# Operands in four transfers, the output weight in four steps and the zero rows in seven pieces, on the load queue of a hybrid decoder layer

## The chip, the core and the metric

The kernel runs on one core of a Trainium2 chip. It is one program in one launch, written in Bass: every engine has its own instruction stream, and semaphores order them. The metric is the device time of one execution in microseconds (us); lower is better.

## The reference, cut to what matters

One decoder layer over 1024 positions of width 1024, all in float32. An input projection feeds three groups of attention heads; their outputs go through one output projection, and a mixture of 32 experts follows.

```python
h = _rmsnorm(x, norm_attn[l])
proj = h @ w_in[l]
...
o_a = _nsa_mixer(nsa_q, kc, vc, ks_, vs_, kw, vw, nsa_g + b_gate[l], ...)
o_b = _fox_mixer(fq, fk, fv, ff + b_fgt[l])
o_c = _diff_mixer(dq, dk, dv, diff_lambda[l], diff_subln[l], _lambda_init(l))
x = x + jnp.concatenate([o_a, o_b, o_c], axis=-1) @ w_out[l]
x = x + _hier_moe(_rmsnorm(x, norm_ffn[l]), ...)
return _rmsnorm(x, norm_final)
```

`_nsa_mixer` has 8 heads with three branches each (compressed, selected, window), `_fox_mixer` 4 heads, `_diff_mixer` 4 heads with two maps each. In every branch a logit is `q . k` over 64 channels (32 in the last group), and a softmax over the allowed keys follows.

## The kernel before, in words

**Stages.** The input projection runs from 0 to about 305 us of the profile, attention from 305 to 733, the output projection with the router to 868, the experts to 1220, and the final gather and norm to the end. The projection is computed in 16 groups of 128 channels. Each group is written transposed to a scratch tensor `T_d` in DRAM, of shape 2 x 16 x 128 x 1024: index 0 holds the high part of each value and index 1 the low part. `T_r` is the same tensor seen as 2 x 2048 x 1024, so that a channel is a row of 4 KB.

**Units.** Attention is cut into 36 units of work in a fixed order: for each of eight heads X (selected), C (compressed) and Y (window), then four F, then eight D (two for each differential head). `PLAN.full` lists the 28 that are not C. The letter f counts them: X and Y alternate in f = 0 to 15, F is f = 16 to 19 and D is f = 20 to 27. Time is cut into slots: a unit X, Y, F or D holds six slots, a unit C one, so a head with X, C and Y takes 13. In a slot TensorE computes scores of the current unit (L1867, L1873, L1874), maxima of a later unit's scores (`max_pass`, L1834), values of an earlier slot (L1893) and at times transposes a row of shifts (`shift_T`, L1845). The maxima of a unit start nine slots before its own scores (`LEAD = 9`): four slots into the unit two before it in `PLAN.full`, and three slots where no C stands between. They need the unit's operands. Its scores need its row of shifts besides.

**Operands.** A unit X, Y or F has four tiles: `Q1`, 128 partitions, with the high part of q on partitions 0 to 63 and the low part on 64 to 127; `K1`, 128 partitions, with the high part of k twice; `Q2` and `K2`, with the high part of q and the low part of k on partitions 0 to 63. They exist three times (`x.set`) and once more for the first unit. `load_unit` fills them from `T_r` by six transfers of 64 rows, 256 KB each. A unit D has two tiles, filled by six transfers of 32 rows. The semaphore `ld_in` of a set counts 16 for each finished transfer, and `loaded(x)` is the count that `max_pass` waits for.

**The load queue.** SyncE (SP) issues all these transfers from one instruction stream, and they stand in one queue. Its loop over `PLAN.full` does, for each f: `shift_row(x)`, which waits for the maxima and then copies the 4 KB row of shifts into `Q2`, and for an X the same for its C; a wait until the unit before x has all its scores, then `load_unit(PLAN.full[f + 2])`; in the second unit of each D head one store of zero rows; and the store `O_d` of a finished head. At f = 4 it issues the output weight `wo` (tile `wraw`), 4 MB, as four transfers in a row. At f = 20 it issues two loads `ot` from `O_d`. `Y_d`, where the experts write, has 19 tiles of 96 rows that may stay unused and must be zero. Each of the four zero stores writes a quarter of the columns of all 19. `wo` is first read in the D units, the zero rows after the experts.

Before attention, one load of operands (the first unit's) and `K1y`, two transfers of 64 rows, stand in the same queue between the projection's stores to `T_d` and a load of projection weight, `wst`. ACT (`wth`, L872) and DVE (`wtl`, L1187) split `wst` before TensorE multiplies it (L1727).

Of the kernel before, what the change touches and what calls it, by code (L numbers as in the profile page):

```python
# [23 lines left out]
SEQ, D = 1024, 1024  # L24
# [3 lines left out]
HD = 64  # L28
# [7 lines left out]
CAP = 96  # L36
MAX_OVF = 2 * SEQ // (CAP + 1)
SURE = 2
NB = NE + SURE
# [141 lines left out]
def program(nc, a, out):  # L181
    f32, f32r = mybir.dt.float32, mybir.dt.float32r
# [4 lines left out]
    with ctx:  # L187
# [18 lines left out]
        def C(n, lo=0, hi=None):  # L206
# [67 lines left out]
        Q1, Q2, K1, K2 = ([at(f"{n}{u}", [P, SEQ], f32r, o + 4 * KB * k) for u, o in enumerate(SETS)]  # L274
                          for k, n in enumerate(("q1_", "q2_", "k1_", "k2_")))
# [11 lines left out]
        zrow = at("zrow", [P, D // 4], f32, ZE + 32 * KB)  # L287
# [3 lines left out]
        wraw = at("wraw", [P, KC, D], f32, ZD + 32 * KB)  # L291
# [60 lines left out]
        T_r = T_d.rearrange("a g p t -> a (g p) t")  # L352
# [3 lines left out]
        Y_d = nc.dram_tensor("Y_d", [NROWS, D], f32).ap()  # L356
# [40 lines left out]
        blk_zero = sem("blk_zero")  # L397
# [22 lines left out]
        yz_st = sem("yz_st")  # L420
# [54 lines left out]
        M_BANK, O_BANK = (4, 6), (5, 7)  # L475

        RS_D, RS_H, RS_K = 4, 5, 13
        ROUTES = ((0, 4, "0"), (4, 6, "1"), (6, 8, "2"))
        A_BATCH = ((0, 1), (1, 1), (2, 2), (4, 4))
        K_BATCH = ((0, 4), (4, 3), (7, 1))  # L480
# [47 lines left out]
        def _(sp_):  # L528
# [54 lines left out]
            def load_unit(x):  # L583

                if x.kind == "D":
                    q0, k0 = (HD * x.head + g * P + 32 * x.u for g in (G_QD, G_KD))
                    for b, (qp, kp_) in enumerate(((0, 0), (1, 0), (0, 1))):
                        for dst, part, r0 in ((Q2, qp, q0), (K2, kp_, k0)):
                            sp_.dma_start(dst[x.set][32 * b:32 * b + 32, :].bitcast(f32), T_r[part, r0:r0 + 32, :])\
                               .then_inc(ld_in[x.set], 16)  # L590
                    return
                if x.kind == "F":
                    q0, k0 = G_QF * P + HD * x.head, G_KF * P + HD * x.head
                else:
                    q0, k0 = G_QN * P + HD * x.head, (G_KS, G_KW)["XY".index(x.kind)] * P + HD * x.g
                for dst, half, part, r0 in ((Q1, 0, 0, q0), (Q1, 1, 1, q0), (K1, 0, 0, k0), (K1, 1, 0, k0),
                                            (Q2, 0, 0, q0), (K2, 0, 1, k0))[4 * (x.n == 2):]:
                    sp_.dma_start(dst[x.set][HD * half:HD * half + HD, :].bitcast(f32), T_r[part, r0:r0 + HD, :])\
                       .then_inc(ld_in[x.set], 16)

            def shift_row(x):
                row = 96 if x.kind in "CD" else HD
# [24 lines left out]
            for p in range(2):  # L627
                sp_.wait_ge(t_st[p], 32 * 8 + 1)

            stored = 0  # L630
            for f, x in enumerate(PLAN.full):
                if f:
                    shift_row(x)
                if f and x.kind == "X":
                    shift_row(PLAN.units[x.n + 1])
                if f >= 2 and f + 2 < len(PLAN.full):
                    sp_.wait_ge(s_ready, PLAN.units[x.n - 1].s_no[-1] + 1)
                    load_unit(PLAN.full[f + 2])
                if x.kind == "D" and x.u == 1:
                    sp_.wait_ge(blk_zero, 3)  # L640
                    c = slice(x.head * (D // 4), (x.head + 1) * (D // 4))
                    sp_.dma_start(Y_d[NB * CAP:, c].rearrange("(n p) d -> p n d", p=CAP),
                                  zrow[0:CAP].unsqueeze(1).broadcast_to([CAP, MAX_OVF - SURE, D // 4]))\
                       .then_inc(yz_st, 16)
                if f and PLAN.full[f - 1].kind in "YF":
                    sp_.wait_ge(oh_ready, stored + 1)
                    sp_.dma_start(O_v[:, :, HD * stored:HD * stored + HD], oh[:, stored % 2])\
                       .then_inc(oh_st[stored % 2], 16)
                    stored += 1
                    if stored == NSA_H + FOX_H:  # L650
                        for p in range(2):
                            sp_.wait_ge(oh_st[p], 16 * stored // 2)
                        for p in range(2):
                            sp_.dma_start(ot[:, p, :], O_d[p * P:(p + 1) * P, :]).then_inc(o_in[p], 16)
                if f == 4:
                    for c in range(4):
                        sp_.dma_start(wraw[:, 2 * c:2 * c + 2, :],
                                      a["wo"][c].rearrange("p (k n) -> p k n", k=2)).then_inc(wo_in, 16)

            def load_expert(e, q):  # L660
                sp_.dma_start(wgu[q][:], a["wgu"][e].rearrange("p (k n) -> p k n", k=KC)).then_inc(we_in[q], 16)
# [61 lines left out]
        def _(pool):  # L723
# [128 lines left out]

            for p in range(2):
                pool.wait_ge(y_st[p], 16 * NB // 2 + 1)
            pool.wait_ge(yz_st, 16 * 4)
            pool.wait_ge(ovf_y, 16 * n_ovf + 1)
            apart(pool)
            for t in range(NT):
# [11 lines left out]
        def _(act):  # L870
# [241 lines left out]
                if n:  # L1112
                    m_out(n - 1)
            m_out(NB - 1)
            act.wait_ge(yz_st, 16 * 4)
            act.wait_ge(y_st[0], 16 * NB // 2 + 1)
            n_ovf = act.value_load(info[0:1, 0:1], min_val=0, max_val=MAX_OVF - SURE)
            with act.Fori(0, MAX_OVF - SURE) as j:
# [573 lines left out]
        def _(pe_):  # L1692
# [112 lines left out]
            spread(5, 6)  # L1805
            def loaded(x):
                f = PLAN.full.index(x)
                return 96 * ((f - 1) // 3 + 1) - 64 * (x.set == 0) if f else 96

            def operands(x):  # L1810
                q1, k1 = (Q1[3], K1y) if x.n == 2 else (Q1[x.set], K1[x.set])
# [378 lines left out]
```

## Time and profile before

| | us |
|---|---|
| median of 3 runs | 1268.73 |
| lowest and highest of them | 1268.67, 1278.55 |
| the profiled execution, its own time | 1273.82 |
| span of its profile | 1271.9 |
| attention, 305 to 733, PE busy | 389.77 of 428.00 |
| experts, 868 to 1220, PE busy | 335.64 of 352.00 |

The span is what the profiler sees from the first to the last instruction; 1.9 us of the profiled execution lie around it. In the profile PE is TensorE's matmuls, PEld its weight loads, SPq the instructions by which SyncE issues transfers, q1 the hardware queue into which they go. PEclk is the granted clock of TensorE as a share of full speed. `q<-shr` is the copy of a row of shifts, `q<-T_d` and `k<-T_d` are loads of operands. The DMA view of a window gives the number of packets that started in it, how many of them are small, and for a queue its packets, MB and the share of 16 engines' time that they took.

### The profile page before, as it was taken

Reading aid. Unit: us, or ns where it says so; the run is one execution under the profiler, and the core shown is the slowest. Engines: PE = TensorE matmul, PEld = TensorE weight load, DVE = VectorE, ACT = ScalarE, POOL = GpSimd, SP = SyncE. Lnnn points to the kernel's source line nnn. Section 1 sums busy time; section 2 is a strip of 40 time slices with the busy share of each in tenths; the row PEclk is TensorE's granted clock in tenths of the full one; section 3 lists DMA queues with packets and bytes.
Section 4 is the critical chain, followed back from the end, with each engine's and each line's share of the span. In section 5 each row is a group of like instructions: output and inputs, shape, how many; then the busy total and the mean of one; then the engine's idle time right before and its main releaser. Section 6 shows DMA issues by size and latency. Waiting matters only on the chain.

```text
span 1271.9 us, 29600 instructions
## 1 busy us (share of the span) xinstructions
PE 1135.7 (89%) x12090; PEld 920.2 (72%) x12090; DVE 615.6 (48%) x1621; ACT 386.1 (30%) x691; POOL 188.0 (15%) x425
## 2 busy tenths in 40 slices
PE   6999899998998999999898889984999999999930
PEld 5989788786776778878676678874777777776710
DVE  4332345334665667665566443456343343344328
ACT  6411122222453555444565522220111111111103
POOL 1110000001211112111262200011110010011033
PEclk9999899999998999899988899996899999999975
DMA  8022654365455555444524343219899999999656
GB/s 338 17 83 97 209 182 149 117 182 146 97 139 185 120 118 118 109 110 95 159 76 141 100 164 103 91 52 358 301 393 377 389 391 378 373 390 386 232 188 258
DMA packets 69381, 251.58 MB, mean 198 GB/s; under 512 B 22176, under 2 KB 30272, under 8 KB 59392
## 3 DMA queue, kind: packets, MB, share of 16 engines
q1 hardware_dynamic: 59328, 219.53, 51.5%
q0 software_dynamic: 6112, 16.79, 3.9%
q10 hardware_dynamic: 3808, 13.37, 2.8%
q8 instruction: 98, 1.61, 0.5%
q14 instruction: 35, 0.29, 0.1%
HBM read 205.34 MB, written 49.15 MB: 200 GB/s over the span
## 4 chain that ended last, share of the span: by engine, by line
PE 75%; DMA 10%; DVE 8%; issue 3%; SPq 2%; ACT 1%; POOL 1%; POOLq 0%; DVEq 0%; ACTq 0%
PE PS L2036 14%; PE PS L1727 12%; PE PS L1893 10%; PE PS L2044 8%; PE PS L1973 7%; PE PS L1716 5%; PE PS L1834 4%; PE PS L1873 4%; PE PS L1874 3%; DMA wdn<-in_wdn 2%; DMA k<-T_d 2%; PE PS L2027 2%; PE PS L1867 2%; DMA q<-shr 2%; DMA wst<-in_wt 1%
## 5 line engine op out<-in xcount | busy, mean ns | idle before, releaser
L1032 ACT ACTIVATE pt<-PS,cst 128x512 f32<-128x512 f32 (+3 forms) x288 | 172.3, 649 | 167.2 <-PE PS L1874 122.2
L2036 PEld LDWEIGHTS PS<-XT,wgu 128*64 128x64 f32 x4352 | 184.5, 139 | 30.3 <-issue 29.3
L2036 PE MATMUL PS<-XT,wgu 128*64 128x96 f32 x4352 | 190.8, 249 | 4.7 <-issue 2.7
L1339 DVE CUSTOM_DVE_ANT_0 junkm<-PS,cst 128x512 f32<-128x512 f32 (+3 forms) x276 | 137.2, 532 | 94.0 <-PE PS L1834 90.9
L1893 PEld LDWEIGHTS PS<-V,pt 128*64 128x64 f32 x3840 | 137.2, 148 | 36.1 <-issue 22.5
L1893 PE MATMUL PS<-V,pt 128*64 128x65 f32 x3840 | 161.0, 237 | 0.0
L2044 PE MATMUL PS<-wdn,aT 128*96 128x512 f32 x272 | 122.5, 593 | 0.9 <-DVE YO L1638 0.9
L790 POOL TENSOR_SCALAR_AFFINE_SELECT pt<-pt 128x128 f32<-128x128 f32 x224 | 67.6, 304 | 269.9 <-ACT pt L1032 221.6
L1727 PE MATMUL PS<-hTh,wth 128*128 128x512 f32 x256 | 103.0, 402 | 4.6 <-DVE wtl L1187 4.6
L1834 PE MATMUL PS<-k,q 128*128 128x128 f32 (+3 forms) x324 | 92.4, 364 | 11.8 <-DMA k<-T_d 6.8
L1727 PE MATMUL PS<-hTh,wtl 128*128 128x512 f32 x256 | 100.7, 393 | 0.0
L1727 PE MATMUL PS<-hTl,wth 128*128 128x512 f32 x256 | 100.7, 393 | 0.0
L1873 PE MATMUL PS<-q,k 128*128 128x512 f32 (+1 forms) x228 | 88.8, 398 | 4.6 <-DMA q<-shr 4.6
L1624 DVE TENSOR_SCALAR ge<-PS 128x192 f32<-128x192 f32 x34 | 12.1, 357 | 160.8 <-PE PS L2036 160.7
L2044 PEld LDWEIGHTS PS<-wdn,aT 128*96 128x96 f32 x272 | 41.7, 163 | 56.1 <-issue 56.0
L1874 PE MATMUL PS<-q,k 65*128 65x512 f32 (+1 forms) x240 | 80.6, 353 | 0.0
L1834 PEld LDWEIGHTS PS<-k,q 128*128 128x128 f32 (+1 forms) x324 | 62.7, 204 | 21.3 <-DMA k<-T_d 7.8
L836 POOL DMA_INDIRECT XG<-h_d,ids x34 | 32.9, 968 | 296.2 <-PE PS L2027 273.6
L1096 ACT ACTIVATE ge<-ge 128x192 f32<-128x192 f32 x34 | 12.3, 363 | 188.6 <-DVE ge L1624 188.6
L1727 PEld LDWEIGHTS PS<-hTh,wth 128*128 128x128 f32 x256 | 48.7, 190 | 16.0 <-DVE wtl L1187 5.1
L1973 PE MATMUL PS<-woh,oth 128*128 128x512 f32 x128 | 51.9, 406 | 5.4 <-DVE otl L1440 4.8
L1727 PEld LDWEIGHTS PS<-hTl,wth 128*128 128x128 f32 x256 | 48.7, 190 | 10.8 <-issue 1.0
(262 smaller groups left out, 1618.2 us busy)
## 6 DMA issues: line engine op xcount, KB each, us to landing
wgu<-in_wgu SPq DMA_DIRECT2D x34, 2048.0 KB, 13.3
wdn<-in_wdn SPq DMA_DIRECT2D x34, 1024.0 KB, 19.6
q<-T_d SPq DMA_DIRECT2D x58, 256.0 KB, 4.7
k<-T_d SPq DMA_DIRECT2D x58, 256.0 KB, 5.6
Y_d<-YO ACTq DMA_DIRECT2D x34, 384.0 KB, 10.1
wst<-in_wt SPq DMA_DIRECT2D x16, 512.0 KB, 6.6
T_d<-thi SPq DMA_DIRECT2D x16, 512.0 KB, 2.6
T_d<-tlo SPq DMA_DIRECT2D x16, 512.0 KB, 3.9
```

The source lines that it names most:

```text
L790: ins = nc.gpsimd.affine_select(out=o, in_=o, compare_op=ALU.is_ge, fill=0.0, base=0, pattern=[[1, P]], channel_multiplier=-1)
L1032: ins = nc.scalar.activation(pt[:, (n + 2) % 6, 0:nt * P], PS[:, n % 4, 0:nt * P], ACT.Exp, scale=C("slopes", h, h + 1), bias=C("kb", w, w ...
L1339: V_.tensor_tensor_reduce(out=junk_[:, 0:L], in0=PS[:, bank, 0:L], in1=tab, scale=1.0, scalar=-3e38, op0=ALU.add, op1=ALU.max, accum_out=m ...
L1716: ins = mm(o, x[:, k, t * P:(t + 1) * P], wv[w][:, k, :], start=(k == 0 and x is hTh and w == 0), stop=(k == KC - 1 and w == 1))
L1727: ins = mm(PS[:, 2 * p + h, :], w[:, p, k * P:(k + 1) * P], x[:, k, h * 512:(h + 1) * 512], start=(k == 0 and w is wth and x is hTh), stop ...
L1834: ins = mm(PS[:, bank, 0:nk * P], q_[:, t * P:(t + 1) * P], k_[:, k0 * P:(k0 + nk) * P], start=True, stop=True)
L1873: mm(o, k1[:, j * P:(j + 1) * P], q1[:, q], start=True, stop=False)
L1874: ins = mm(o, k2[0:HD + 1, j * P:(j + 1) * P], q2[0:HD + 1, q], start=False, stop=True)
L1893: ins = mm(PS[h * HD:(h + 1) * HD, O_BANK[b % 2], (t % 4) * VW:(t % 4 + 1) * VW], pt[0:rows, (n + 2) % 6, q * P + h * HD:q * P + (h + 1) * ...
L1973: ins = mm(PS[:, 2 + h, :], x[:, t % 2, k, :], w[:, k, h * 512:(h + 1) * 512], start=(k == 0 and x is oth and w is woh), stop=(k == KC - 1 ...
L2036: ins = mm(PS[h * HD:(h + 1) * HD, 2 + p, f * CAP:(f + 1) * CAP], wgu[q][:, c, lo:lo + HD], XT[:, p, c, :], start=(c == 0 and f == 0), sto ...
L2044: ins = mm(PS[0:CAP, 5 + h, :], aT[:, p, c, :], wdn[q][:, c, h * 512:(h + 1) * 512], start=(c == 0), stop=(c == 1))
```

## The change

Three things change on SP's queue, and the counts that others wait for follow.

1. For X, Y and F, `Q1` is loaded by one transfer whose source is `T_r[:, q0:q0 + HD, :]`, 2 x 64 x 1024, and `K1` by one whose source is the 64 rows of k under a leading dimension of 2 with step 0. Both write 128 partitions. `Q2` and `K2` keep a transfer of 64 rows each. So 19 units take four transfers, not six. The first Y takes `Q2` and `K2` alone, as before; D units keep their six.
2. The output weight is issued in four steps of 1 MB, one in each of f = 4 to 7, after that unit's load.
3. The zero rows are stored in seven pieces of two or three tiles, one in each of f = 8 to 14, after that unit's load, and none in the D units.

```diff
                 else:
                     q0, k0 = G_QN * P + HD * x.head, (G_KS, G_KW)["XY".index(x.kind)] * P + HD * x.g
-                for dst, half, part, r0 in ((Q1, 0, 0, q0), (Q1, 1, 1, q0), (K1, 0, 0, k0), (K1, 1, 0, k0),
-                                            (Q2, 0, 0, q0), (K2, 0, 1, k0))[4 * (x.n == 2):]:
-                    sp_.dma_start(dst[x.set][HD * half:HD * half + HD, :].bitcast(f32), T_r[part, r0:r0 + HD, :])\
+                if x.n != 2:
+                    sp_.dma_start(Q1[x.set][:].bitcast(f32), T_r[:, q0:q0 + HD, :])\
                        .then_inc(ld_in[x.set], 16)
+                    sp_.dma_start(K1[x.set][:].bitcast(f32),
+                                  T_r[0:1, k0:k0 + HD, :].broadcast_to([2, HD, SEQ])).then_inc(ld_in[x.set], 16)
+                sp_.dma_start(Q2[x.set][0:HD, :].bitcast(f32), T_r[0, q0:q0 + HD, :]).then_inc(ld_in[x.set], 16)
+                sp_.dma_start(K2[x.set][0:HD, :].bitcast(f32), T_r[1, k0:k0 + HD, :]).then_inc(ld_in[x.set], 16)
...
+            def zero_rows(i):
+
+                n0, n1 = (NB + (MAX_OVF - SURE) * j // ZERO for j in (i, i + 1))
+                sp_.wait_ge(blk_zero, 3)
+                sp_.dma_start(Y_d[n0 * CAP:n1 * CAP, :].rearrange("(p r) (q d) -> p (r q) d", p=CAP, q=4),
+                              zrow[0:CAP].unsqueeze(1).broadcast_to([CAP, 4 * (n1 - n0), D // 4])).then_inc(yz_st, 16)
...
-                if x.kind == "D" and x.u == 1:
-                    sp_.wait_ge(blk_zero, 3)
-                    c = slice(x.head * (D // 4), (x.head + 1) * (D // 4))
-                    sp_.dma_start(Y_d[NB * CAP:, c].rearrange("(n p) d -> p n d", p=CAP),
-                                  zrow[0:CAP].unsqueeze(1).broadcast_to([CAP, MAX_OVF - SURE, D // 4]))\
-                       .then_inc(yz_st, 16)
+                if f in range(4, 8):
+                    sp_.dma_start(wraw[:, 2 * f - 8:2 * f - 6, :],
+                                  a["wo"][f - 4].rearrange("p (k n) -> p k n", k=2)).then_inc(wo_in, 16)
+                if f in range(8, 8 + ZERO):
+                    zero_rows(f - 8)
...
-                if f == 4:
-                    for c in range(4):
-                        sp_.dma_start(wraw[:, 2 * c:2 * c + 2, :],
-                                      a["wo"][c].rearrange("p (k n) -> p k n", k=2)).then_inc(wo_in, 16)
...
             def loaded(x):
                 f = PLAN.full.index(x)
-                return 96 * ((f - 1) // 3 + 1) - 64 * (x.set == 0) if f else 96
+                before = [y for y in PLAN.full[1:f + 1] if y.set == x.set]
+                return 16 * sum({"D": 6}.get(y.kind, 2 if y.n == 2 else 4) for y in before) if f else 64
```

The waits for the zero rows change from 16 x 4 to 16 x 7 in the same way.

The first place is SP's queue around the output weight, f = 4. `q_2_108` and `k_2_116` are `Q1` and `K1` of set 2, `q_2_112` and `k_2_120` its `Q2` and `K2`. Before:

```order
L605 DMA q_0_110<-shr 1x8x128 x2
L598 DMA q_2_108<-T_d 64x1024 x2
L598 DMA k_2_116<-T_d 64x1024 x2
L598 DMA q_2_112<-T_d 64x1024
L598 DMA k_2_120<-T_d 64x1024
L647 DMA O_d<-oh 128x8x64
L657 DMA wraw<-in_wo 128x2048 x4
L605 DMA q_1_111<-shr 1x8x128
```

After:

```order
L609 DMA q_0_110<-shr 1x8x128 x2
L598 DMA q_2_108<-T_d 128x1x1024
L600 DMA k_2_116<-T_d 128x1x1024
L602 DMA q_2_112<-T_d 64x1024
L603 DMA k_2_120<-T_d 64x1024
L651 DMA wraw<-in_wo 128x2048
L657 DMA O_d<-oh 128x8x64
L609 DMA q_1_111<-shr 1x8x128
```

The two pairs of 64-row transfers have become two transfers of 128 rows, and three quarters of the weight no longer stand ahead of the next row of shifts.

The second place is SP's queue around f = 8, the first with a piece of zero rows. Before:

```order
L605 DMA q_1_111<-shr 1x8x128 x2
L598 DMA q_0_106<-T_d 64x1024 x2
L598 DMA k_0_114<-T_d 64x1024 x2
L598 DMA q_0_110<-T_d 64x1024
L598 DMA k_0_118<-T_d 64x1024
L647 DMA O_d<-oh 128x8x64
L605 DMA q_2_112<-shr 1x8x128
```

After:

```order
L609 DMA q_1_111<-shr 1x8x128 x2
L598 DMA q_0_106<-T_d 128x1x1024
L600 DMA k_0_114<-T_d 128x1x1024
L602 DMA q_0_110<-T_d 64x1024
L603 DMA k_0_118<-T_d 64x1024
L638 DMA Y_d<-zrow 768x1x256
L657 DMA O_d<-oh 128x8x64
L609 DMA q_2_112<-shr 1x8x128
```

A store of 768 pieces of 1 KB now stands between the unit's load and the next row of shifts.

## Rows read from the trace of the kernel before

**Rows 1.** The page's chain that ended last, shares of the span.
```profile
PE 75%; DMA 10%; DVE 8%; issue 3%; SPq 2%; ACT 1%; POOL 1%; POOLq 0%; DVEq 0%; ACTq 0%
```

**Rows 2.** Two windows: busy time by engine, then PEclk, DMA share, GB/s.
```profile
305.00:733.00 428.00, 389.77 (x5163) 318.28 (x5162) 266.62 (x1010) 216.48 (x363) 103.64 (x281) 0.92 0.49 125
...
390.50:397.40 6.90, 6.50 (x57) 5.20 (x58) 3.21 (x13) 2.47 (x4) 1.17 (x4) 0.61 0.78 183
```

**Rows 3.** Waits of PE, 305 to 733: total, times, longest.
```profile
PE PS L1834 <- DMA k<-T_d: 6.8, 4, 3.9
...
PE PS L1867 <- DMA q<-shr: 6.4, 3, 4.0
...
PE PS L1873 <- DMA q<-shr: 4.6, 1, 4.6
```

**Rows 4.** PE's timeline, six places: start, duration, idle time before in brackets.
```profile
326.38 0.33 PE L1873 MATMUL PS<-q,K1y 128*128 128x128 f32 x1
...
390.90 0.48 PE L1873 MATMUL PS<-q,k 128*128 128x128 f32 x1 [4.61 <-DMA q<-shr]
...
554.55 0.33 PE L1834 MATMUL PS<-k,q 128*128 128x128 f32 x1 [1.43 <-DMA k<-T_d]
...
570.83 0.33 PE L1834 MATMUL PS<-k,q 128*128 128x128 f32 x1 [1.12 <-DMA k<-T_d]
...
584.89 0.33 PE L1834 MATMUL PS<-k,q 128*128 128x128 f32 x1 [0.33 <-DMA k<-T_d]
...
631.79 1.22 PE L1867 MATMUL PS<-q,k 97*128 97x512 f32 x2 [4.00 <-DMA q<-shr]
```

**Rows 5.** SP's timeline, the first issue of seven loads of operands.
```profile
253.17 1.98 SPq L598 DMA_DIRECT2D q<-T_d  x2
...
304.31 0.80 SPq L598 DMA_DIRECT2D q<-T_d  x1
...
438.43 1.14 SPq L598 DMA_DIRECT2D q<-T_d  x2
...
468.96 1.14 SPq L598 DMA_DIRECT2D q<-T_d  x2
...
544.99 1.24 SPq L598 DMA_DIRECT2D q<-T_d  x2
...
560.93 1.09 SPq L598 DMA_DIRECT2D q<-T_d  x2
...
575.78 1.10 SPq L598 DMA_DIRECT2D q<-T_d  x2
```

**Rows 6.** DMA in 480.7:483.4, 226:241, 590:595, 276:286 (q1), 452.8:464.
```profile
DMA packets 16, 0.00 MB, mean 2 GB/s; under 512 B 8, under 2 KB 16, under 8 KB 16
...
DMA packets 433, 1.58 MB, mean 105 GB/s; under 512 B 48, under 2 KB 48, under 8 KB 432
...
DMA packets 290, 0.81 MB, mean 162 GB/s; under 512 B 96, under 2 KB 96, under 8 KB 288
...
q1 hardware_dynamic: 288, 1.05, 26.2%
...
DMA packets 482, 1.60 MB, mean 143 GB/s; under 512 B 96, under 2 KB 96, under 8 KB 480
...
q1 hardware_dynamic: 480, 1.57, 61.7%
```

**Rows 7.** DMA in 743:756, and a small load's issue to landing.
```profile
q1 hardware_dynamic: 144, 0.52, 11.8%
...
pe<-in_pe SPq DMA_DIRECT2D x1, 16.0 KB, 1.9
```

**Rows 8.** ACT, DVE and PE around the next projection weight.
```profile
267.14 1.06 ACT L872 ACTIVATE wth<-wst 128x1024 fp32r<-128x1024 f32 x1 [2.25 <-DMA wst<-in_wt]
...
268.23 1.23 DVE L1187 TENSOR_TENSOR wtl<-wst,wth 128x1024 fp32r<-128x1024 f32 x1 [2.55 <-ACT wth L872]
...
276.10 0.79 PE L1727 MATMUL PS<-hTh,wth 128*128 128x512 f32 x1
```

More of the change, by code:

```diff
@@ L477, in program @@
         RS_D, RS_H, RS_K = 4, 5, 13
+        ZERO = 7
         ROUTES = ((0, 4, "0"), (4, 6, "1"), (6, 8, "2"))
@@ L854, in _ @@
                 pool.wait_ge(y_st[p], 16 * NB // 2 + 1)
-            pool.wait_ge(yz_st, 16 * 4)
+            pool.wait_ge(yz_st, 16 * ZERO)
             pool.wait_ge(ovf_y, 16 * n_ovf + 1)
@@ L1114, in _ @@
             m_out(NB - 1)
-            act.wait_ge(yz_st, 16 * 4)
+            act.wait_ge(yz_st, 16 * ZERO)
             act.wait_ge(y_st[0], 16 * NB // 2 + 1)
```

## The prediction

> **What bounds the kernel now.** I read the chain of waits first, then the windows by stage, then PE's waits in attention, then the timelines of PE and SP around them, and last the DMA counts of short windows. The chain says that matmuls set the end for 75% of the span and transfers for 10% [rows 1]. All three parts of the change act in attention, so only that stage counts. There PE is busy 389.77 of 428 us, at a mean granted clock of 0.92 [rows 2]. What the change can reach is the time in which PE waits for the load queue: 6.8 us in four waits for a unit's operands, 6.4 us in three waits for a row of shifts in the D units, and 4.6 us in one such wait behind the output weight [rows 3]. That is 17.8 us, plus what the clock loses after a long wait: in the 6.9 us behind the 4.61 us gap at 390.9 PEclk is 0.61 [rows 2, 4], so 0.39 x 6.9 = 2.7 us of work. I take 2.7 us for each wait of about 4 us or more.
>
> **How long a unit's load may take.** The load for f + 2 is issued when unit f starts, and PE wants it three slots later (four where a C lies between). For the last three X/Y/F loads the issues are at 544.99, 560.93 and 575.78 [rows 5], PE stood ready 1.43, 1.12 and 0.33 us before 554.55, 570.83 and 584.89 [rows 4], so it got there after 8.1, 8.8 and 8.8 us, and the loads took 9.6, 9.9 and 9.1 us. A head of 13 slots lasts 468.96 - 438.43 = 30.5 us [rows 5], 2.35 us a slot, so where a C lies between PE gets there after 8.6 + 2.35 = 10.9 us. This is the number to beat: a load slower than that is paid for in full, once for each unit, since the load behind it is not issued before the next unit starts.
>
> **Part 1, four transfers for six: how wide is a transfer?** The bytes are the same. What changes is the shape. Short windows of the DMA view tell how the queue cuts one. A row of shifts alone has 16 packets, 8 of them under 512 B; its 4 KB are described as 8 pieces, so 8 data packets and 8 small closing ones. Three transfers of 128 rows make 432 + 1 packets with 48 small ones, 16 each; six of 32 rows have 96 small ones, 16 each again [rows 6]. One closing packet for each DMA engine used fits all: 16 engines where the outermost count is 128 or 32, 8 where it is 8. The new sources have an outermost count of 2: two halves of `T_r` for `Q1`, a dimension of 2 with step 0 for `K1`. By this pattern each runs on 2 engines, though it writes 128 partitions. That is my choice for the sum, against a reading by the destination alone.
>
> The Trainium skill says the same as a rule, in "DMA: Bandwidth & Descriptors", section "Why a DMA increments its semaphore by 16 and not by 1": the number of engines is the largest up to 16 that divides the slowest non-1 dimension of both sides. The section "Rules for kernel authors" of that page names a leading zero-stride broadcast as the case that confines a transfer. By this rule the row of shifts has 8 and the new loads 2; the trace shows the 8, and nothing in it shows a 2.
>
> The pace of one engine: two stores of 128 rows keep 16 engines 26.2% of 10 us busy for 256 packets of 4 KB [rows 6], 0.164 us each. A load of 128 rows gives 11.8% of 13 us for 128 packets [rows 7], 0.192 us. The present loads of 64 rows give 61.7% of 11.2 us for 384 packets [rows 6], 0.288 us. Each of the two engines would move 64 packets for `Q1`, 64 for `K1` and 4 each for `Q2` and `K2`, 136 in all. I take 0.164 us, because only two engines run and nothing crowds them: 22.3 us, and 1.9 us from issue to landing of a load that is almost nothing [rows 7]. One unit's load: **24.2 us**.
>
> Now the sum. (a) Loads issued in f = 2 to 14: 24.2 - 10.9 + 2.7 = 16.0 us, 13 times, 208 us. (b) f = 15, 16, 17, which waited already: 24.2 less 9.6, 9.9 and 9.1, plus 2.7 each, 52 us. (c) The start: from 304.31 [rows 5] the two engines have the first Y's 8 packets and two loads of 136; the first Y's row of shifts stands behind them and lands at 304.3 + 1.9 + 280 x 0.164 = 352.1. PE began that unit at 326.38 [rows 4]: 25.7 us, and 2.7 for a second slow stretch. (d) The first unit's load at 253.17 [rows 5] stands ahead of `K1y` (8 packets) and `wst` (8) on those engines: 253.2 + 1.9 + 152 x 0.164 = 280.0, then 1.06 us for `wth` and 1.23 for `wtl`, 282.3 where PE went on at 276.10 [rows 8]: 6.2 us. SP saves some 1.2 us of issue in each unit, which nobody waits for: SP stands idle before each row of shifts. Part 1 costs 208 + 52 + 28.4 + 6.2 = **295 us**.
>
> The same skill, in "SBUF — State Buffer", section "Door 1: The DMA port swizzle", says that 64 partitions reach only half of the ports, and in "DMA: Bandwidth & Descriptors", section "Rules for kernel authors", that one transfer of 128 partitions beats two of half. The 0.288 against 0.164 us a packet agrees. Taken alone, this rule makes the change a gain; it is the first rival.
>
> **Part 2, the weight in four steps.** Three of its 4 MB no longer stand ahead of the row of shifts at f = 5. The wait of 4.6 us goes, and its slow stretch: -7.3 us. The pieces at f = 5, 6 and 7 cost nothing: 1 MB is 16 packets of 4 KB an engine, 2.6 us behind a load of 24.2, with the next load some 30 us later. Its reader comes in the D units, 200 us later. If the loads stayed short, 1 MB would land 2.6 us behind a load of 9 us, still inside the 15 us of a unit.
>
> **Part 3, the zero rows.** In the D units two waits go, 6.4 less the longest of 4.0 [rows 3], -2.4 us. The 4.0 us one ends at 631.79 [rows 4], in the first D units, where `ot` and `O_d` stand ahead of the row of shifts and no zero store has gone out; it stays. The seven pieces cost nothing for the reason given under part 2.
>
> Sum: 295 - 7.3 - 2.4 = 285 us. Against the profiled execution that is 1273.8 + 285 = 1559; that execution is 5.1 us over the median of the runs, so **1554 us**.
>
> **The rivals.** *Sixteen engines* (ends faster). If the destination's 128 partitions set the width, a unit has 16 packets an engine at 0.164 and 8 at 0.288, 4.9 us in place of 6.9. Then all four waits for operands go, 6.8 us with two slow stretches (5.4), though only the 3.9 us one is long; I count one stretch, 2.7. With parts 2 and 3: 6.8 + 2.7 + 7.3 + 2.4 = 19 us, 1250 us, between 1242 (more slow stretches go) and 1262 (VectorE is late next). The width decides: from 4 engines on a load (128 / 4 x 0.164 + 8 x 0.288 + 1.9 = 9.4 us) ends within 10.9 us. For it speaks that `wst` and all other loads of 128 partitions run on 16; against it, that none of them has a source cut differently from its destination. *Two engines at the crowded pace.* If reading `T_d` itself is what costs 0.288 us, a load takes 136 x 0.288 + 1.9 = 41.1 us: 16.9 us more in 16 units, 35 us more at the start, 19 in the projection, 1878 us. Against it: the packets differ between 64 and 128 partitions, not between tensors. *The change does less than it says*: the order of SP's instructions shows it done, so the only form of this is the first rival.
>
> **How the numbers follow.** Two engines near 0.164 us: 0.80, 1554 us. Crowded pace: 0.07. Sixteen engines: 0.13, of which 0.02 within 1%. About 1% is what a measurement of this kernel can tell from no change. The range: without any loss of clock, 18 x 2.7 = 49 us less, and a slot more of slack in some units, 1490; at 0.192 us a packet 61 us in the units, 8 at the start, 4 in the projection, and a full half clock for 6.9 us (0.75 us more each), 1640. The other cases lie far outside and hold 0.20.
>
> **What the profile of the changed kernel would show.** Right: `q<-T_d` and `k<-T_d` of 512 KB that land after 12 to 24 us; a window with one such load with 2 small packets for each of its two wide transfers; a DMA share near 0.15 through attention; PE waiting some 13 us in each of 16 units, for `k<-T_d` or `q<-T_d`; a head of about 62 us; no wait of PE for a row of shifts at f = 5; the stages from 733 on unchanged in length. Wrong: wide loads that land in 5 us, 16 small packets each, PE busy above 0.93 in attention. With 4 or 8 small packets a transfer the time would lie near the first rival's.

## The result and the profile after

The changed kernel takes 1593.65 us (median of 4 runs, 1590.67 to 1597.07) against 1269.30 (4 runs, 1268.67 to 1278.55): a ratio of 1.2535, 95% interval 1.2471 to 1.2599. It is a quarter slower. Its profiled execution took 1595.02 us, with a span of 1593.1.

The page first: PE's busy time, then the chain that ended last by engine and by line.

```profile
PE 1184.2 (74%) x12090; PEld 956.1 (60%) x12090; DVE 617.5 (39%) x1621; ACT 386.4 (24%) x691; POOL 187.8 (12%) x425
...
PE 54%; DMA 24%; SPq 13%; DVE 5%; issue 3%; ACT 1%; POOL 1%; POOLq 0%; DVEq 0%; ACTq 0%
DMA k<-T_d 18%; PE PS L2043 11%; SPq L602 10%; PE PS L1733 9%; PE PS L2051 7%; PE PS L1980 6%; PE PS L1900 5%; PE PS L1722 4%; PE PS L1841 3%; DMA wdn<-in_wdn 2%; PE PS L2034 2%; DMA q<-shr 1%; PE PS L1874 1%; DMA wst<-in_wt 1%; PE PS L1880 1%
```

The chain answers to [rows 1]: PE fell from 75% to 54%, transfers rose from 10% to 24%, and SPq from 2% to 13%. Two entries are new and large, the load `k<-T_d` and SP's own issue of a load in L602 (`Q2`). PE did the same 12090 matmuls in 1184.2 us, not in 1135.7; the lower granted clock behind the waits, shown below, accounts for the 48.5 us.

PE's waits from 300 to 1054 us, the attention stage of the changed kernel (L1841 is the old L1834, L1874 and L1880 are L1867 and L1873):

```profile
PE PS L1841 <- DMA k<-T_d: 260.8, 17, 18.4
```

These answer to [rows 3]. The wait for a unit's operands went from 6.8 us in 4 to 260.8 us in 17. That is one for each of the sixteen units loaded in f = 2 to 17, and one at the start.

PE's timeline at five places:

```profile
287.46 0.77 PE L1733 MATMUL PS<-hTh,wth 128*128 128x512 f32 x1 [11.95 <-issue]
...
369.89 0.47 PE L1880 MATMUL PS<-q,K1y 128*128 128x128 f32 x1 [14.83 <-DMA q<-shr]
...
415.72 0.80 PE L1841 MATMUL PS<-k,q 128*128 128x128 f32 x2 [16.28 <-DMA k<-T_d]
...
910.13 0.48 PE L1841 MATMUL PS<-k,q 128*128 128x128 f32 x1 [17.93 <-DMA k<-T_d]
...
956.93 0.73 PE L1874 MATMUL PS<-q,k 97*128 97x512 f32 x2 [1.37 <-DMA q<-shr]
```

They answer to [rows 4] and [rows 8]. The projection's matmul of 276.10 comes at 287.46, the first Y of 326.38 at 369.89, the last X/Y/F maxima of 584.89 at 910.13. The row of shifts behind the weight, a wait of 4.61 us before, is not waited for: the only wait of L1880 is the first Y's. The one at f = 21 went from 4.00 to 1.37.

SP's timeline of one load (f = 2), the DMA view inside it, 391.5 to 398.9 us, and the packets of the whole next load (f = 3), 422.6 to 449.6 us:

```profile
389.30 0.55 SPq L598 DMA_DIRECT2D q<-T_d  x1
389.90 0.53 SPq L600 DMA_DIRECT2D k<-T_d  x1
390.47 7.90 SPq L602 DMA_DIRECT2D q<-T_d  x1
398.41 0.60 SPq L603 DMA_DIRECT2D k<-T_d  x1
```

```profile
q1 hardware_dynamic: 94, 0.39, 12.9%
...
DMA packets 437, 1.59 MB, mean 59 GB/s; under 512 B 44, under 2 KB 52, under 8 KB 436
```

Ninety-four packets of 4 KB in 7.4 us, at 12.9% of 16 engines, are two engines (12.5%) that never pause, at 0.16 us a packet (two engines x 7.4 us / 94). The second row has 44 small packets: 16 each for `Q2` and `K2` and 8 for the row of shifts make 40, which leaves two for each wide transfer. The four issues should take 0.6 us each; the third takes 7.90. That is what put SPq into the chain. In f = 8 to 14, where a piece of zero rows follows the load, SP's next issue behind the piece (`O_d` or a row of shifts) is held as well, for 5.9 to 12.0 us in six of the seven. From the first issue at 389.30 to PE's start at 415.72 the load takes 26.4 us.

Windows: a busy stretch and a waiting one, then two stretches behind waits, then the stage behind attention. Columns as in [rows 2].

```profile
391.00:399.00 8.00, 8.00 (x127) 6.77 (x126) 5.43 (x23) 4.51 (x8) 1.17 (x4) 1.00 0.13 52
440.00:448.00 8.00, 0.00 (x0) 0.00 (x0) 0.00 (x0) 0.00 (x0) 0.00 (x0) 0.50 0.13 51
...
415.70:419.70 4.00, 3.98 (x37) 3.46 (x37) 1.01 (x5) 0.70 (x2) 0.07 (x1) 0.50 0.02 4
...
453.50:457.50 4.00, 4.00 (x24) 2.75 (x24) 2.47 (x9) 1.67 (x3) 0.56 (x2) 0.50 0.09 33
...
1054.00:1189.00 135.00, 121.98 (x663) 104.40 (x662) 61.74 (x143) 28.98 (x65) 10.61 (x43) 0.94 0.33 121
```

The transfer share is 0.13 in both of the first two stretches, whether PE works or waits: two engines of 16. In the waiting stretch no engine computes. The granted clock is 0.50, the lower of its two levels (1.2 GHz), in the last part of the wait and in the stretches behind it. Over the 12 us behind each of the sixteen waits it is 0.59 to 0.86, so the lower level lasts 3.4 to 9.8 us there. The stages after attention are 135 and 352 us long as before: all of the loss lies ahead of 1054.

### The profile page after: what moved, and what is told of

Read it like the earlier page. It is cut to its first block, busy times and chain, and to the rows that moved or that the text cites. A ratio compares the mean times of both kernels' runs of the same rounds, so it can differ in the third digit from the quotient of the medians.

```text
span 1593.1 us, 29565 instructions
## 1 busy us (share of the span) xinstructions
PE 1184.2 (74%) x12090; PEld 956.1 (60%) x12090; DVE 617.5 (39%) x1621; ACT 386.4 (24%) x691; POOL 187.8 (12%) x425
## 4 chain that ended last, share of the span: by engine, by line
PE 54%; DMA 24%; SPq 13%; DVE 5%; issue 3%; ACT 1%; POOL 1%; POOLq 0%; DVEq 0%; ACTq 0%
DMA k<-T_d 18%; PE PS L2043 11%; SPq L602 10%; PE PS L1733 9%; PE PS L2051 7%; PE PS L1980 6%; PE PS L1900 5%; PE PS L1722 4%; PE PS L1841 3%; DMA wdn<-in_wdn 2%; PE PS L2034 2%; DMA q<-shr 1%; PE PS L1874 1%; DMA wst<-in_wt 1%; PE PS L1880 1%
## 5 line engine op out<-in xcount | busy, mean ns | idle before, releaser
L1841 PE MATMUL PS<-k,q 128*128 128x128 f32 (+3 forms) x324 | 104.0, 402 | 266.0 <-DMA k<-T_d 260.8
L1841 PEld LDWEIGHTS PS<-k,q 128*128 128x128 f32 (+1 forms) x324 | 67.6, 226 | 280.1 <-DMA k<-T_d 266.2
L1900 PE MATMUL PS<-V,pt 128*64 128x65 f32 x3840 | 177.0, 252 | 0.0
L1900 PEld LDWEIGHTS PS<-V,pt 128*64 128x64 f32 x3840 | 151.8, 161 | 40.7 <-issue 23.6
L1733 PE MATMUL PS<-hTh,wth 128*128 128x512 f32 x256 | 103.1, 403 | 16.4 <-issue 11.9
L1880 PE MATMUL PS<-q,k 128*128 128x512 f32 (+1 forms) x228 | 95.0, 422 | 0.0
L1881 PE MATMUL PS<-q,k 65*128 65x512 f32 (+1 forms) x240 | 87.4, 381 | 0.0
L1630 DVE TENSOR_SCALAR ge<-PS 128x192 f32<-128x192 f32 x34 | 12.2, 358 | 162.2 <-PE PS L2043 162.2
L1345 DVE CUSTOM_DVE_ANT_0 junkm<-PS,FX 128x512 f32<-128x512 f32 (+3 forms) x48 | 25.5, 556 | 88.8 <-PE PS L1844 74.1
L1881 PEld LDWEIGHTS PS<-q,k 65*128 65x128 f32 x240 | 54.2, 226 | 3.7 <-issue 0.2
```

What stands on the lines that cost most here:

```text
L1345: V_.tensor_tensor_reduce(out=junk_[:, 0:L], in0=PS[:, bank, 0:L], in1=tab, scale=1.0, scalar=-3e38, op0=ALU.add, op1=ALU.max, accum_out=m ...
L1733: ins = mm(PS[:, 2 * p + h, :], w[:, p, k * P:(k + 1) * P], x[:, k, h * 512:(h + 1) * 512], start=(k == 0 and w is wth and x is hTh), stop ...
L1841: ins = mm(PS[:, bank, 0:nk * P], q_[:, t * P:(t + 1) * P], k_[:, k0 * P:(k0 + nk) * P], start=True, stop=True)
L1880: mm(o, k1[:, j * P:(j + 1) * P], q1[:, q], start=True, stop=False)
L1881: ins = mm(o, k2[0:HD + 1, j * P:(j + 1) * P], q2[0:HD + 1, q], start=False, stop=True)
L1900: ins = mm(PS[h * HD:(h + 1) * HD, O_BANK[b % 2], (t % 4) * VW:(t % 4 + 1) * VW], pt[0:rows, (n + 2) % 6, q * P + h * HD:q * P + (h + 1) * ...
```

## The experiments

All ratios are to the kernel before, run on the same chip: 1272.39 us (17 runs, 1268.86 to 1277.62) beside the first four kernels, 1272.43 (17 runs, 1266.25 to 1278.49) beside the others.

### widths: one transfer at a time, by the shape of its source

```python
one(T["whole"][:], wt[0])
one(T["sixteen"][:], wt[0:16, 0:P // 16, :])    # eight, four, two in the same way
one(T["twins"][:], wt[0:1, 0:HD, :].broadcast_to([2, HD, SEQ]))
one(T["pairs"][:], wt[0, 0:HD, :].unsqueeze(1).broadcast_to([HD, 2, SEQ]))
one(T["half"][0:HD, :], wt[1, 0:HD, :])
...
sp_.dma_start(T["fst"][:], wt[0:2, 0:HD, :]).then_inc(late, 16)
sp_.dma_start(T["snd"][:], wt[2:4, 0:HD, :]).then_inc(late, 16)
sp_.dma_start(T["trd"][0:HD, :], wt[5, 0:HD, :]).then_inc(late, 16)
```

> Leaves the whole layer out: SP alone loads 512 KB tiles one after another, each waited for, with sources whose outermost count is 128, 16, 8, 4 and 2, twice over, then the step-0 source of the change (2 x 64) and the same rows as 64 x 2, a load of 64 rows and one of 32. Width theory: at 0.16 us a 4 KB packet and some 2 us of fixed time, 16 and 128 land in about 3.3 us, 8 in 4.6, 4 in 7.1, 2 in 12.2; the step-0 source of 2 x 64 in 12.2, the 64 x 2 one in 3.3 to 4.5. Rival (the destination sets the width, and the time of the change comes from the size or from reading T_d): all of 512 KB land within 1 us of each other. Then a 4 KB row behind a wide load and behind a narrow one: by the width theory it lands about 3 us after its issue in the first case, 10 to 12 in the second. Last, two narrow loads and a third load in a row: if SP's long third issue is the queue being full, the third issue takes about 8 us here too, with nothing else going on.

SP's timeline, the second round and what follows it; each transfer of the round is waited for before the next is issued, so the distance to the next row is its time from issue to landing.

```profile
58.27 0.35 SPq L197 DMA_DIRECT2D whole<-in_wt  x1
61.64 0.58 SPq L197 DMA_DIRECT2D sixteen<-in_wt  x1
66.15 0.66 SPq L197 DMA_DIRECT2D eight<-in_wt  x1
72.57 0.56 SPq L197 DMA_DIRECT2D four<-in_wt  x1
81.06 0.52 SPq L197 DMA_DIRECT2D two<-in_wt  x1
93.75 0.51 SPq L197 DMA_DIRECT2D twins<-in_wt  x1
106.23 0.57 SPq L197 DMA_DIRECT2D pairs<-in_wt  x1
109.94 0.51 SPq L197 DMA_DIRECT2D half<-in_wt  x1
113.29 0.34 SPq L197 DMA_DIRECT2D quarter<-in_wt  x1
...
115.97 0.29 SPq L197 DMA_DIRECT2D brow<-in_wt  x1
118.94 0.56 SPq L213 DMA_DIRECT2D bnarrow<-in_wt  x1
119.55 0.48 SPq L197 DMA_DIRECT2D brow<-in_wt  x1
131.69 0.51 SPq L217 DMA_DIRECT2D fst<-in_wt  x1
...
132.80 8.39 SPq L219 DMA_DIRECT2D trd<-in_wt  x1
156.25 18.81 SPq L197 DMA_DIRECT2D out<-whole  x8
```

The packets of `two`, 81 to 93.7 us, and those from 131.0 to 131.3 us:

```profile
DMA packets 130, 0.52 MB, mean 41 GB/s; under 512 B 2, under 2 KB 2, under 8 KB 130
...
DMA packets 5, 0.01 MB, mean 27 GB/s; under 512 B 3, under 2 KB 3, under 8 KB 5
```

The same 512 KB into the same 128 partitions take 3.4 us from 128 source rows, 8.5 from a source whose outermost dimension is 4, and 12.7 and 12.5 where it is 2, as two halves of a tensor (`two`) or as a dimension with step 0 (`twins`). With 64 outermost and the step of 0 inside (`pairs`) they take 3.7. So it is the source's outermost dimension, not the destination's partitions, and the price is what two engines take: 64 x 0.164 + 1.9 = 12.4 us. Two of the 130 packets of `two` are small, one closing packet for each engine. The Trainium skill says of `two` and `twins` what the rows show ("DMA: Bandwidth & Descriptors", section "Why a DMA increments its semaphore by 16 and not by 1"): the number of engines must divide the slowest dimension of both sides.

Three things stand beside this. A 4 KB row behind a wide transfer lands within 3.0 us (115.97 to 118.94). Behind a narrow one it takes 11.5 to 12.1: SP waits for both transfers, until 131.69, and the only small packets of the two, two of the narrow transfer and one of the row, start between 131.0 and 131.3, against the row's issue at 119.55. A third transfer behind two narrow ones holds SP for 8.39 us in its issue, though nothing else runs: the same hold as in L602. With those 64 rows behind them the two narrow transfers have all landed 24.6 us after the first issue (131.69 to 156.25).

### interleaved: the same four transfers on 16 engines

```diff
-                    sp_.dma_start(Q1[x.set][:].bitcast(f32), T_r[:, q0:q0 + HD, :])\
+                    sp_.dma_start(Q1[x.set][:].bitcast(f32), T_r[:, q0:q0 + HD, :].rearrange("a c t -> c a t"))\
...
-                                  T_r[0:1, k0:k0 + HD, :].broadcast_to([2, HD, SEQ])).then_inc(ld_in[x.set], 16)
+                                  T_r[0, k0:k0 + HD, :].unsqueeze(1).broadcast_to([HD, 2, SEQ]))\
```

Channel c now lies on partitions 2c and 2c + 1 instead of c and c + 64; `K1y` (now one transfer, not two) and the compressed keys, which meet the same `Q1`, are laid out the same way, with four more small matmuls and two more small copies on ACT.

> The changed kernel with the same four transfers of the same bytes, but Q1, K1 and K1y hold their 128 partitions as 64 channels x 2 (high and low, or twice the same), so that the outermost count of each source is 64. The compressed keys follow the new order of channels. Width theory: 16 engines, a unit's load lands in some 5 us, no wait of PE for operands, 1250 us, between 1242 and 1262. Rival (a large transfer is slow by itself, or SP's long issue holds the rows back): near 1590 us, as the changed kernel.

1257.49 us (5 runs), ratio 0.9879, interval 0.9854 to 0.9903. The page's issues (KB each, median us to landing), then PE's waits from 305 to 760 us:

```profile
q<-T_d SPq DMA_DIRECT2D x19, 512.0 KB, 4.1
k<-T_d SPq DMA_DIRECT2D x19, 512.0 KB, 5.5
```

```profile
PE PS L1845 <- DMA k<-T_d: 3.0, 2, 2.9
```

For a unit these are the same bytes, the same number of transfers and the same partitions: 336 us faster than the changed kernel and 1.2% faster than the one before. The width is the whole loss. With it restored, the change is the gain that the prediction's first rival gave (1250, from 1242 to 1262).

### steps_only: parts 2 and 3 without part 1

Six transfers a unit as before; the weight in four steps and the zero rows in seven pieces, as in the diff of the change.

> The kernel before with the output weight in four steps and the zero rows in seven pieces, the loads still six transfers of 64 rows. My sum says -7.3 us for the weight and -2.4 for the zero rows: 1259 us, ratio 0.992. Rival (pieces between the units delay rows of shifts or loads): 1269 or above, with new waits of PE for q<-shr or k<-T_d in f = 8 to 14.

1266.01 us (12 runs, 1257.83 to 1269.86), ratio 0.9943, interval 0.9922 to 0.9964. No wait for a row of shifts is left behind the weight. There is now one wait of 0.9 us for POOL's `pt`, and waits for operands are 7.3 us in 5 (4.0 the longest), 6.8 before. At f = 21 PE waits 1.08 us where it waited 4.00, and one wait for a row of shifts, of 1.75 us at 707.14, is left in the D units.

### q1_narrow: only Q1 on two engines

```diff
-                    sp_.dma_start(K1[x.set][:].bitcast(f32),
-                                  T_r[0:1, k0:k0 + HD, :].broadcast_to([2, HD, SEQ])).then_inc(ld_in[x.set], 16)
+                    for half in range(2):
+                        sp_.dma_start(K1[x.set][HD * half:HD * half + HD, :].bitcast(f32), T_r[0, k0:k0 + HD, :])\
+                           .then_inc(ld_in[x.set], 16)
```

> The changed kernel with K1 loaded by two transfers of 64 rows again, so that only Q1 comes by a narrow one: 64 packets on two engines, not 128. Width theory: a load lands in 1.7 + 10.1 + 4.6 = 16.4 us, 5.5 over what PE allows, so with the clock 8 us more in each of 13 units, 10 in three, 12 at the start: about 1405 us, near the middle between 1259 and 1594. Rival (the step 0 of K1's source is what is slow): near 1260 us. Rival (any narrow transfer stops SP's queue): near 1590.

1451.74 us (2 runs), ratio 1.1406, interval 1.1366 to 1.1446: some 47 us over what I expected. The first issue of two loads on SP (f = 5, beside a piece of the weight, and f = 8, without one) and PE's start behind each:

```profile
444.64 0.55 SPq L598 DMA_DIRECT2D q<-T_d  x1
...
521.33 0.53 SPq L598 DMA_DIRECT2D q<-T_d  x1
```

```profile
465.61 0.80 PE L1842 MATMUL PS<-k,q 128*128 128x128 f32 x2 [8.86 <-DMA k<-T_d]
...
539.93 0.79 PE L1842 MATMUL PS<-k,q 128*128 128x128 f32 x2 [7.76 <-DMA k<-T_d]
```

They take 21.0 and 18.6 us. The four loads beside pieces of the weight take 20.3 to 21.0, the other twelve 18.4 to 19.2, not the 16.4 of my count of packets. Half the narrow bytes cost 57% of the loss (0.1527 of 0.2656 in ratio, counted from interleaved), where the expectation had 44% (1405 of 1259 to 1594). The likely reason is that transfers which run at the same time slow these packets, as the longer loads beside the weight show; for the other twelve it is not tested. In the units no issue of the load's own transfers is long. SP is held at the start, behind two narrow transfers (11.95 us at 317.08, a half of `K1`), and for 5.5 to 8.7 us at four stores `O_d` that stand behind a piece of zero rows with one narrow transfer ahead. In interleaved, with the same pieces, no issue of SP between 245 and 760 us takes over 2.5 us.

### part1_only: part 1 without parts 2 and 3

The loads of the changed kernel; the weight at once at f = 4 and the zero rows in the D units, as before.

> The kernel before with part 1 alone: the four narrow transfers of a unit; the output weight goes out at once at f = 4 and the zero rows in the D units, as before. Theory (parts 2 and 3 only pay where loads are short; under loads of 27 us their waits lie in PE's wait for operands, and the pieces of the weight at f = 4 to 7 even lengthen the loads beside them by 1 to 2 us): 1588 to 1596 us, the same as the change within its scatter; the load at f = 5 to 7 takes 26 to 27 us from its first issue to PE's start, not 28 to 29, with one longer one behind the 4 MB of the weight. Rival (the parts add up, as the prediction's sum had it): 1594 + 7.3 + 2.4 = 1603 us, with a wait of PE for a row of shifts of 4 us or more at f = 5.

1596.00 us (4 runs, 1588.57 to 1597.74), ratio 1.2531, interval 1.2492 to 1.2569: the changed kernel's time. SP's issue of the weight and of the next load (f = 5), and PE's start behind it:

```profile
464.79 13.02 SPq L660 DMA_DIRECT2D wraw<-in_wo  x4
...
488.88 0.54 SPq L597 DMA_DIRECT2D q<-T_d  x1
```

```profile
515.13 0.80 PE L1838 MATMUL PS<-k,q 128*128 128x128 f32 x2 [11.19 <-DMA k<-T_d]
```

The loads at f = 5, 6 and 7 take 26.3, 26.6 and 26.7 us, in the changed kernel 29.1, 28.1 and 28.2: the pieces of the weight lengthen the load beside them by 1.5 to 2.8 us. All sixteen loads have a mean of 26.7 us here, against 26.9 in the changed kernel. The wait for the row of shifts at f = 5 is 0.92 us, not 4 or more. The additive sum (1603) falls with it: under loads of 27 us parts 2 and 3 give nothing that can be measured, within the 0.3 to 0.6% of the two intervals.

### interleaved_only: the wide loads without parts 2 and 3

> The kernel before with Q1 and K1 loaded by one transfer each whose source has 64 rows outermost and the two parts inside them; the weight in one go and the zero rows in the D units, as before. Theory (the wide loads take 4 to 5 us instead of 9 and remove only the waits for operands; parts 2 and 3 take the 4.6 us wait behind the weight by themselves): ratio to before 0.992 to 0.996, about 1264 us; steps alone gave 0.994 and both together 0.988, so the two add up. PE still waits 4 us for the row of shifts at f = 5, and hardly for k<-T_d. Rival (the two gains are the same one, a queue less full): 0.988, 1257 us, as with both.

1267.64 us (12 runs, 1262.09 to 1272.07), ratio 0.9955, interval 0.9935 to 0.9976. PE's wait behind the weight, from 380 to 400 us, is as long as before:

```profile
PE PS L1881 <- DMA q<-shr: 4.3, 1, 4.3
```

A wait for operands of 2.95 us stands at 553.84, which I had not expected. 0.9955 x 0.9943 is 0.9898, against 0.9879 with both and an interval that holds it. On short loads the two gains add: some 6 us from the wide transfers, some 7 from parts 2 and 3.

### q2_first: the changed kernel with Q2 and K2 issued first

```diff
+                sp_.dma_start(Q2[x.set][0:HD, :].bitcast(f32), T_r[0, q0:q0 + HD, :]).then_inc(ld_in[x.set], 16)
+                sp_.dma_start(K2[x.set][0:HD, :].bitcast(f32), T_r[1, k0:k0 + HD, :]).then_inc(ld_in[x.set], 16)
                 if x.n != 2:
...
-                sp_.dma_start(Q2[x.set][0:HD, :].bitcast(f32), T_r[0, q0:q0 + HD, :]).then_inc(ld_in[x.set], 16)
-                sp_.dma_start(K2[x.set][0:HD, :].bitcast(f32), T_r[1, k0:k0 + HD, :]).then_inc(ld_in[x.set], 16)
```

> The changed kernel with Q2 and K2 issued ahead of the wide-destination loads Q1 and K1; nothing else moves. Theory (two 64-row transfers on 16 engines crowd the first narrow one or wait behind both of them on the two engines; with them first, the two engines have only Q1 and K1 left, which end together): a load takes 24.5 to 26 us from its first issue to PE's start instead of 26.9, so 1560 to 1585 us; SP's 8 us issue goes away, since no third transfer meets the two narrow ones before the row of shifts. Rival (the load is the two engines' 128 to 136 packets whatever the order): 1594 us within 0.5%. In both, if the long issue moves to the row of shifts behind the load, it is the third transfer after two narrow ones that holds SP, whatever it is.

1556.39 us (4 runs, 1551.88 to 1562.37), ratio 1.2254, interval 1.2217 to 1.2292. Nothing but the order differs, and 37 us are back. SP's timeline of the load at f = 4 with its piece of the weight, then PE's start behind it and behind the load at f = 8:

```profile
445.00 0.50 SPq L597 DMA_DIRECT2D q<-T_d  x1
...
446.79 0.53 SPq L602 DMA_DIRECT2D k<-T_d  x1
447.37 9.09 SPq L651 DMA_DIRECT2D wraw<-in_wo  x1
...
570.04 0.50 SPq L597 DMA_DIRECT2D q<-T_d  x1
```

```profile
471.41 0.80 PE L1841 MATMUL PS<-k,q 128*128 128x128 f32 x2 [15.36 <-DMA k<-T_d]
...
594.51 0.79 PE L1841 MATMUL PS<-k,q 128*128 128x128 f32 x2 [11.44 <-DMA k<-T_d]
```

The hold of 9.09 us moved to the piece of weight, the first transfer behind the two narrow ones. In nine of the eleven loads behind which a piece of the weight or of the zero rows follows at once, that piece is held for 8.1 to 9.3 us, in the other two (f = 12 and 13) for 2.1 and 2.2. A load takes 25.0 us in the mean of the sixteen (26.4 here, beside a piece of the weight; 24.5 at f = 8), against 26.9 in the changed kernel.

### interleaved_moved: two moves on SP's queue for what is left

The interleaved kernel, with the load for f = 2 (the second head's X) ahead of that for f = 1 (the first Y), and the two loads `ot` one unit later, behind that unit's load.

```diff
-            for x in PLAN.full[1:4]:
+            for x in (PLAN.full[2], PLAN.full[1], PLAN.full[3]):
...
+                if f == 21:
+                    for p in range(2):
+                        sp_.wait_ge(oh_st[p], 16 * stored // 2)
+                    for p in range(2):
+                        sp_.dma_start(ot[:, p, :], O_d[p * P:(p + 1) * P, :]).then_inc(o_in[p], 16)
...
```

> The interleaved kernel (16 engines for Q1 and K1, weight in four steps, zero rows in seven pieces), with two moves on SP's queue: at the start the load of the first X ahead of that for the Y before it, and the two loads ot from O_d moved one unit later, behind that unit's load. Theory (the two waits that are left in attention, 2.9 us for k<-T_d at 315 us and 1.1 us for the row of shifts at f = 21, come from what stands ahead in the queue): 1251 to 1254 us, 4 to 6 us below the interleaved kernel. Rival (another engine is late next there, or the wait for the first Y's operands takes the place): 1257 us, no difference.

1255.51 us (4 runs, 1253.45 to 1256.91), ratio 0.9872, interval 0.9845 to 0.9898. The intervals of the two interleaved kernels overlap nearly whole, so a gain is not shown. PE's starts on the maxima of f = 2, interleaved and then moved, each with a later wait for a row of shifts:

```profile
315.04 0.50 PE L1845 MATMUL PS<-k,q 128*128 128x128 f32 x2 [2.86 <-DMA k<-T_d]
...
695.88 0.73 PE L1878 MATMUL PS<-q,k 97*128 97x512 f32 x2 [1.74 <-DMA q<-shr]
```

```profile
315.25 0.49 PE L1845 MATMUL PS<-k,q 128*128 128x128 f32 x2 [2.44 <-DMA k<-T_d]
...
693.40 0.73 PE L1878 MATMUL PS<-q,k 97*128 97x512 f32 x2 [1.69 <-DMA q<-shr]
```

The load for f = 2 was issued 1.5 us earlier (303.16, not 304.64), and PE still starts at the same time. Ten transfers go out within 7 us there; why the place among them did not decide was not tested. The wait of 1.1 us at f = 21 is gone with `ot` moved. The one of 1.7 us for a later row of shifts was there before the move and stays.

## Why the prediction was right, and where it was off

The forecast was 1554 us in a range of 1490 to 1640; the kernel takes 1593.65. Its main mechanism held: the new sources run on two engines, and each unit pays for it in full. It was 40 us low, and by the profiles the sum was 285 where 321.2 was found (1593.1 - 1271.9). By its own steps:

| stretch | predicted | measured |
|---|---|---|
| up to the first Y's scores, (c) and (d) | +34.6 | 369.89 - 326.38 = +43.5 |
| from there to the last wait for operands, (a), (b), part 2 | 208 + 52 - 7.3 = +252.7 | 910.13 - 584.89 - 43.5 = +281.7 |
| the rest, part 3 | -2.4 | -4.0 |

**Width** (right). Two engines, from the count of closing packets: DMA share 0.13, and a transfer alone takes 12.5 us. The pace of 0.164 us a packet was right too, 0.16 here. Choosing it over the crowded 0.288 decided between 1554 and 1878. The new shape in a trace could be told from the closing packets of the old ones.

**The load, 24.2 us** (mis-sized). It measured 26.9, the mean of 16 from first issue to PE's start (25.6 to 29.1; 26.4 at f = 2). The term holds for the two engines alone: in widths two narrow transfers and 64 rows behind them, on a chip with nothing else to do, landed in 24.6 us. The prediction had nothing for what the transfers beside them cost. q2_first gives 1.8 of the 2.7 us back by order alone; where the rest goes is open. The pieces of the weight account for 1.5 to 2.8 us of three loads, but hardly for the mean, which is 26.7 without them (part1_only). The step that said that these pieces "cost nothing" under a load of 24.2 us was wrong all the same. In q1_narrow loads were 2.0 to 4.6 us over the count of packets.

**The clock, 2.7 us for each long wait** (mis-sized, and right in total by luck). PE's busy time rose by 48.5 us, 18 x 2.7 = 49 predicted. But the mean clock in the 12 us behind the sixteen waits is 0.715, which is 3.4 us of work lost at each, and the 48.5 us are a net: the slow stretches behind the waits of the kernel before (0.61 behind 390.9) are in its busy time.

The longer loads did not come through in full either: 16 x 2.7 us make 43, but PE's waits in the sixteen units are 242 us where the sum had 217 (13 x 13.3 and, for the last three, 44). The difference lies in what PE does between a load's first issue and its wait. The sum had 10.9 us for f = 2 to 14; it measures 12.4 in the mean. Two rows of the kernel before (448.32, behind the issue of 438.43) and of the changed one (481.08 less the wait, behind the issue of 453.45):

```profile
448.32 0.40 PE L1834 MATMUL PS<-k,q 128*128 128x128 f32 x2
```

```profile
481.08 0.80 PE L1841 MATMUL PS<-k,q 128*128 128x128 f32 x2 [14.82 <-DMA k<-T_d]
```

That is 9.9 us before and 12.8 after. For even f, where the next load goes out 3.9 us behind PE's start (449.57, 453.45) and so within the slow stretch, it was 9.9 to 10.1 us before and is 12.2 in the mean of f = 4 to 14. For odd f, where it goes out 6.7 to 8.2 us behind (415.72, 422.63), it was 12.7 in the mean (without f = 5, which has the wait of 4.61 us in it) and is 13.0 for f = 3 to 13. What PE loses beside a load only shortens the next wait. This is read from the two traces; no run tests it.

**The start** (mis-sized). The wait for the projection's weight cost 11.4 us, not 6.2 (287.46 against 276.10). I had counted packets and left SP out: its third issue took 8.06 us at 254.07, so the issue of `wst` came at 265.88 instead of 259.04. When SP is free again the two engines are still full, so how the 5.2 us over the prediction divide between the late issue and the crowd is not settled. Then the loads and the first Y's row behind them took 52.8 us (317.09 to 369.89) against 47.8 predicted; one issue of SP there is held for 17.09 us.

**"SP stands idle"** (wrong). The 1.2 us of issue saved in each unit became 8 us of being held, and L602 stands in the chain with 10%. In the units it seems to cost little by itself: in q2_first a hold as long remains, in another place, with loads near 24.5 us. No run takes the hold away and leaves the two narrow transfers, so what it costs is not shown.

**Part 2** (right on short loads, void here). steps_only removes the wait of 4.6 us and gains 0.6% (0.4 to 0.8) with part 3; under narrow loads nothing of it can be measured. In a sum, a gain that lives on slack must be struck out where the slack is filled with a longer wait.

**Part 3 and f = 21** (wrong on a small point). I said that the 4.0 us wait would stay, since no zero store stands ahead of it. It is 1.37 after the change, 1.08 with parts 2 and 3 alone, and gone in interleaved_moved. So `ot` ahead of the row is one cause. But the wait is also 1.33 in interleaved_only and 0.88 in part1_only, which store the zero rows as before. So it is not part 3 that took the 3 us off; what made the wait that long in the one profile of the kernel before, the runs do not tell. Of the two waits that were to go, 2.4 us, one of 0.58 is left in the changed kernel and one of 1.75 in steps_only.

**What the profile would show**: small packets, share near 0.15, waits near 13 us in each of 16 units, later stages unchanged: found (two small packets for each wide transfer; 0.13 while only the wide transfers run, 0.25 in the mean from 300 to 1054; 242 us in 16, or 15.1 each). A head takes 65.2 us (389.30 to 780.52 on SP for six heads), not 62.

**The rivals.** Sixteen engines did not happen, and the run in which they do is interleaved: 1257.49 against 1250 named. Of its threshold ("from 4 engines on") widths says that it was too kind: 512 KB on four engines take 8.5 us for `Q1` alone, where 32 packets at 0.164 and the 1.9 us make 7.1.

## What to carry to other kernels

Before joining transfers, look at the outermost dimension of the source as it is written: 2 x 64 rows into 128 partitions run at an eighth of the width, and turning the same access to 64 x 2 cost another order of partitions, which must then hold for all tiles that meet in a contraction, and here four small matmuls and two copies. In a trace, a share stuck at n/16 while every engine waits is the sign, and the closing packets of existing transfers tell the width before a new one is tried. Count what shares those engines too, and take a long issue on the queue's sequencer as another sign: here it came only with narrow transfers outstanding.

## What the runs showed of the hardware that was not expected

- A third transfer behind two that use two engines holds the issuing engine: 7.90 us in the kernel, 8.39 alone on the chip, 9.09 when it is another transfer. With one narrow transfer ahead the issues of 64 rows take 0.6 us (q1_narrow), but `O_d` behind a piece of zero rows is held there for 5.5 to 8.7. In the five kernels without narrow transfers no issue from 245 us to the end of attention takes over 2.5 us.
- 512 KB into 128 partitions take, in the second round of widths, 3.4 us from 128 rows, 4.5 from 16 x 8, 6.4 from 8 x 16, 8.5 from 4 x 32, 12.7 from 2 x 64. A source of 16 x 8 is slower than one of 128, though both can run on 16 engines, and the pace per packet on four or eight engines is worse than on two: (8.5 - 1.9) / 32 = 0.21 and (6.4 - 1.9) / 16 = 0.28 us. Why is open.
- 64 rows (256 KB) alone take 3.4 us, as long as 128 rows. The Trainium skill, in "DMA: Bandwidth & Descriptors", section "Rules for kernel authors", asks for one transfer of 128 partitions in place of two halves; these rows agree.
- The granted clock fell to 0.50 in waits of 12 to 18 us and stayed there for 3.4 to 9.8 us of full work behind them. For f = 2 PE stops at 399.4; the clock is 0.98 from 402 to 404 and 0.50 from 404 on.
